# Holding GpSimd back from the values' block until six of the eight normed tiles have their residues

## The chip, the cores and the metric

The kernel runs on one core of a Trainium2 chip. The metric is the device time of one launch in microseconds. Before the change it was 2746.05 us, the median of three runs (2745.25 to 2750.39). The engines that matter here are TensorE (matmuls, PE in the rows), VectorE (DVE), ScalarE (ACT), GpSimd (POOL) and SyncE, which issues the loads (SP).

## The reference, cut to what matters

Two small transformer blocks run one after the other on 512 rows of width 1024, with a context of 256 rows. The change lies at their seam: the last norm of the first block, the modulation of the second block's first layer, and the keys, values and queries of its windowed attention.

```python
def rmsnorm(x, g):
    xf = x.astype(jnp.float32)
    inv = lax.rsqrt(jnp.mean(xf * xf, axis=-1, keepdims=True) + RMS_EPS)
    return (xf * inv).astype(x.dtype) * g
...
    return rmsnorm(x, final_g)            # end of the first block
...
        hx = x * (1.0 + sc1) + sh1
        hc = ctx * (1.0 + csc1) + csh1
...
    q = apply_rope((hx @ wq).reshape(B, L, A_KV_HEADS, G, HEAD_DIM), cos, sin)
    k = apply_rope((hx @ wk).reshape(B, L, A_KV_HEADS, HEAD_DIM), cos, sin)
    v = (hx @ wv).reshape(B, L, A_KV_HEADS, HEAD_DIM)
    kc = (hc @ wk).reshape(B, C, A_KV_HEADS, HEAD_DIM)
    vc = (hc @ wv).reshape(B, C, A_KV_HEADS, HEAD_DIM)
```

## The kernel before, in words

**Products in three parts.** Each float32 product is done as three matmuls on a faster format: every operand is split into a rounded part (hi) and a residue (lo), and hi x hi, lo x hi and hi x lo are summed. The activations live transposed, eight tiles of 128 features by 768 columns (512 rows of x, then 256 of the context), in `Ahi` and `Alo`. The weights stream from HBM in blocks of 128 x 2048, two halves each, into a ring of three slots (`raw`); GpSimd splits each half into `whi` and `wlo` with a multiply (L526) and a subtract (L528). SyncE loads a half into a slot as soon as TensorE has used the half that was there (semaphore `w_used`). The order of blocks on GpSimd is written out by hand in its own program.

**The norm "n5".** VectorE adds the last products of the feed-forward network into X, ScalarE squares X, TensorE sums the squares (L708), ScalarE and VectorE form the root and its inverse (L1342, L1758), and TensorE spreads it over the partitions into PSUM (L718). Then, for k from 0 to 8, VectorE issues in this order: tile k scaled, its 512 columns (L1778, one input from PSUM) and its 256 context columns (L2101, SBUF to SBUF); and the residues of tile k - 1 (L1785, two SBUF inputs, one instruction for 512 and one for 256 columns), for which ScalarE has meanwhile written the rounded part (L1367). The semaphore `n5_out`, on the semaphore that all norms share as `out`, counts the tiles whose residues are written. TensorE's key product (block `B_KV`) waits for it tile by tile. After the eighth tile VectorE goes on, in its own order, with eight pairs of scalings of X (L2106, SBUF to SBUF, and L2107, with an input from PSUM), and with the rotations of the two key heads.

**What follows.** TensorE's key product runs over 8 tiles with the first block of keys (two heads), then the values' product with the block `B_KV + 1`, which needs both halves of that block split. ScalarE copies the keys' halves in swapped order (L1326), and VectorE rotates each head with three instructions: L2113 (an input from PSUM), L2115 and L2118 (two SBUF inputs). When both rotations and ScalarE's copy of the values are done (semaphore `kvA_evac` at 3), TensorE transposes the values (L1040), VectorE copies them out of PSUM (L2128), and only then the query product with the blocks from `B_WQA` starts.

**The places touched.** GpSimd's program calls `split_run(B_KV, ring_end(B_WOA))`: it splits the keys' block, the values' block and five blocks behind them, each as soon as its half has landed. Block `B_KV` has slot 2 of the ring, the values' block slot 0, the first query block slot 1.

Of the kernel before, what the change touches and what calls it, by code (L numbers as in the profile page):

```python
# [28 lines left out]
KT = D // P  # L29
# [87 lines left out]
B_KV = B_FF[1] + FF_BLOCKS  # L117
B_WQA = B_KV + 2
B_WOA = B_WQA + 4
# [50 lines left out]
def build(nc, ins, out):  # L170
    ctx = ExitStack()
    with ctx:
# [51 lines left out]
        def sem(name):  # L224
            name = shared.get(name, (name, 0))[0]
            if name not in sems:
                sems[name] = ctx.enter_context(nc.semaphore(name))
            return sems[name]

        def when(name, count):  # L230

            return sem(name), count + shared.get(name, (name, 0))[1]
# [287 lines left out]
        def _(pool):  # L520
            def split(s, half, loaded, nth):

                part = slice(half * HALF, (half + 1) * HALF)
                pool.wait_ge(*when(f"raw{s}{half}", loaded))
                pool.sem_inc(sem("w_turn"), 1)
                pool.tensor_scalar(whi[:, s, part], raw[:, s, part], 1.0, 1.0, ALU.mult, ALU.mult).then_inc(sem("w_hi"), 1)  # L526
                pool.wait_ge(*when("w_hi", nth))
                pool.tensor_tensor(wlo[:, s, part], raw[:, s, part], whi[:, s, part], ALU.subtract).then_inc(sem("w_split"), 1)  # L528

            def split_block(b, more=0, rounds=0):  # L530

                for half in range(2):
                    split(b % RING, half, 16 * rounds + (16 * (b // RING) + 16), more + (SPLITS[b] + half + 1))

            def split_run(first, end):

                a, z = -(-first // RING), end // RING
                if z - a < 2:
                    for b in range(first, end):
                        split_block(b)  # L540
                    return
                for b in range(first, a * RING):
                    split_block(b)
                with pool.Fori(0, z - a) as i:
                    for s in range(RING):
                        split_block(a * RING + s, 2 * RING * i, i)
                for b in range(z * RING, end):
                    split_block(b)

            def split_swiglu(f):  # L550
                B0 = B_FF[f]
                for b in (B0 + 2, B0 + 3):
                    split_block(b)
                with pool.Fori(0, FF_IT // 3) as p:
                    for s in range(3):
                        for b in (0, 2, 4):
                            split_block(B0 + 4 + 5 * s + b, FF_SPLITS * p, 5 * p)
                for i in range(FF_IT // 3 * 3, FF_IT - 1):
                    for b in (0, 2, 4):
                        split_block(B0 + 4 + 5 * i + b)  # L560
                split_block(B0 + FF_BLOCKS - 1)

            def ring_end(b):
                return -(-b // RING) * RING
# [53 lines left out]
            split_swiglu(0)  # L618
            split_block(B_POOL)
            split_swiglu(1)  # L620
            split_run(B_KV, ring_end(B_WOA))
            for u in range(N_UNITS):
                pool.wait_ge(*when("denA", u + 1))
                prob = probA[u % 4][:, 1:1 + len(keys(UNITS[u][2])) * P]
# [44 lines left out]
        def _(pe):  # L669
# [34 lines left out]
            def quarters(bank, cols, src, k):  # L704

                n = sum(n for _, n in cols) // 4
                for q in range(4):
                    mm = pe.matmul(ps[32 * q:32 * q + 32, bank, 0:n], ones[:, 0:32], src[:, q * n:(q + 1) * n],  # L708
                                   start=(k == 0), stop=(k == KT - 1), skip_group_check=True)
                return mm  # L710

            def spread(bank, cols, src):

                n = sum(n for _, n in cols) // 4
                for q in range(4):
                    a, z = q * n, (q + 1) * n
                    for c0, c1 in ((a, z),) if a // 512 == (z - 1) // 512 else ((a, 512), (512, z)):
                        mm = pe.matmul(psf[:, bank * 512 + c0:bank * 512 + c1], ident[:, 32 * q:32 * q + 1].to_broadcast([P, P]),  # L718
                                       src[:, c0 - a:c1 - a], start=True, stop=True, skip_group_check=True)
                return mm  # L720
# [21 lines left out]
            def dense(name, b0, cols, ready, first_two=True):  # L742


                slots = 8 // len(cols)
                dst = [[ps[:, (j % slots) * len(cols) + c, 0:n] for c, (_, n) in enumerate(cols)] for j in range(8)]
                blocks = [(SPLITS[b0 + i], b0 + i) for i in range(4)]
                for i in ((0, 2, 3) if ready else range(4)):
                    both = bool(ready) and i == 0
                    if 2 * i + 2 > slots:  # L750
                        pe.wait_ge(*when(f"{name}_evac", 2 * i + 2 - slots))
                    columns(f"{name}_done", blocks[i:i + 1 + both], cols, dst[2 * i:], ready if both else None)
# [1753 lines left out]
```

## Time and profile before

| | |
|---|---|
| median of 3 runs | 2746.05 us (2745.25 to 2750.39) |
| the profiled execution, its own time | 2749.13 us |
| its span | 2747.3 us |
| TensorE busy | 2598.0 us, 95% of the span |
| VectorE busy | 1489.6 us, 54% |
| GpSimd busy | 1357.1 us, 49% |
| ScalarE busy | 649.7 us, 24% |
| mean granted clock of TensorE | 0.973 of full speed |

The span runs from the first to the last instruction of the profiled execution; its own time is the device time of that same execution. The busy shares are means over the whole program. The change concerns some 60 us of it, around 1005 to 1065 us, and the rows below are read there: timelines of single engines, with the start, the length and the line of each instruction, and the chain of waits, which follows the work that ended last.

### The profile page before, as it was taken

To read this page: it belongs to the slowest core of one execution; us is meant where nothing else is said; L and a number is where in the kernel's file an instruction comes from. 1 tells how busy PE (TensorE), PEld (TensorE's weight loads), DVE (VectorE), ACT (ScalarE), POOL (GpSimd) and SP (SyncE) were. 2 spreads that over 40 slices of the span, in tenths; PEclk is the share of its full clock that TensorE was granted. 3 is DMA by queue.
4 is the path that set the end of the run, shared out by engine and by line. 5 is a ranking of instruction groups with operands and counts; after the bars stand their busy time and mean duration, and the time that the engine had idled before them with its cause. 6 is when DMAs were issued, how large, how long until landed. Compare 5 with 4: busy or idle time off the path is not lost.

```text
span 2747.3 us, 39149 instructions
## 1 busy us (share of the span) xinstructions
PE 2598.0 (95%) x14176; PEld 2103.1 (77%) x14176; DVE 1489.6 (54%) x2473; ACT 649.7 (24%) x1220; POOL 1357.1 (49%) x880
## 2 busy tenths in 40 slices
PE   7989999989999989889989999999799999899997
PEld 6668777777777768656768888888588887688885
DVE  7945666466566645354454333333676665544444
ACT  2220000041000023567131111111255552211112
POOL 6374565536555554133546444444252525766661
PEclk9999999999999999999999999999899999999998
DMA  5124444434444431000111112111011111232321
GB/s 196 47 78 146 153 153 153 151 118 133 153 153 153 153 123 62 31 1 1 47 39 62 61 63 67 61 61 61 31 47 46 43 34 56 69 98 92 99 92 46
DMA packets 67387, 235.73 MB, mean 86 GB/s; under 512 B 8144, under 2 KB 9552, under 8 KB 67152
## 3 DMA queue, kind: packets, MB, share of 16 engines
q1 hardware_dynamic: 65792, 233.64, 26.1%
q8 instruction: 63, 1.03, 0.2%
q10 hardware_dynamic: 1488, 0.69, 0.1%
q14 instruction: 44, 0.36, 0.0%
HBM read 232.21 MB, written 2.10 MB: 85 GB/s over the span
## 4 chain that ended last, share of the span: by engine, by line
PE 87%; DVE 6%; ACT 3%; issue 2%; POOL 1%; DMA 1%; SPq 0%; DVEq 0%; ACTq 0%; POOLq 0%
PE ps L675 70%; PE ps L1210 2%; PE ps L1233 2%; PE ps L830 2%; PE ps L1172 2%; PE ps L1098 1%; PE ps L1084 1%; PE ps L794 1%; PE ps L1164 1%; PE ps L708 1%; DVE Alo L1785 1%; PE ps L718 1%; DVE tmp L1778 1%; DMA raw<-in_stream 1%; DVE X L1796 1%
## 5 line engine op out<-in xcount | busy, mean ns | idle before, releaser
L526 POOL TENSOR_SCALAR whi<-raw 128x1024 fp32r<-128x1024 f32 x332 | 372.8, 1123 | 1024.4 <-DMA raw<-in_stream 1024.2
L528 POOL TENSOR_TENSOR wlo<-raw,whi 128x1024 fp32r<-128x1024 f32 x332 | 804.3, 2423 | 27.7
L675 PE MATMUL ps<-Ahi,whi 128*128 128x512 f32 (+1 forms) x2128 | 726.6, 373 | 41.6 <-DVE Alo L1785 18.7
L675 PE MATMUL ps<-Alo,whi 128*128 128x512 f32 (+1 forms) x2128 | 719.4, 369 | 0.0
L675 PE MATMUL ps<-Ahi,wlo 128*128 128x512 f32 (+1 forms) x2128 | 717.1, 368 | 0.0
L2222 DVE SCALAR_TENSOR_TENSOR X<-ps,modT,X 128x512 f32<-128x512 f32 (+1 forms) x384 | 242.4, 659 | 504.7 <-PE ps L675 504.7
L675 PEld LDWEIGHTS ps<-Ahi,whi 128*128 128x128 f32 x2128 | 374.9, 190 | 121.3 <-DVE Alo L1785 19.2
L675 PEld LDWEIGHTS ps<-Ahi,wlo 128*128 128x128 f32 x2128 | 374.6, 190 | 68.9
L675 PEld LDWEIGHTS ps<-Alo,whi 128*128 128x128 f32 x2128 | 375.6, 190 | 66.6 <-issue 0.7
L675 PE MATMUL ps<-hhi,whi 128*128 128x512 f32 x1120 | 375.9, 373 | 9.2 <-DVE hlo L2212 8.4
L675 PE MATMUL ps<-hhi,wlo 128*128 128x512 f32 x1120 | 374.8, 372 | 0.0
L675 PE MATMUL ps<-hlo,whi 128*128 128x512 f32 x1120 | 372.5, 369 | 0.0
L675 PEld LDWEIGHTS ps<-hhi,whi 128*128 128x128 f32 x1120 | 193.9, 189 | 53.5 <-DVE hlo L2212 9.2
L675 PEld LDWEIGHTS ps<-hlo,whi 128*128 128x128 f32 x1120 | 193.7, 189 | 39.1
L675 PEld LDWEIGHTS ps<-hhi,wlo 128*128 128x128 f32 x1120 | 193.6, 189 | 39.0
L1326 ACT ACTIVATE hhi<-tmp 128x512 fp32r<-128x512 f32 (+1 forms) x108 | 73.6, 695 | 633.3 <-DVE tmp L2208 472.6
L1994 DVE TENSOR_TENSOR X<-ps,X 128x512 f32<-128x512 f32 x176 | 121.7, 691 | 139.8 <-PE ps L675 139.8
L1970 DVE SCALAR_TENSOR_TENSOR ps<-raw,arena,ps 128x256 f32<-128x256 f32 x432 | 173.9, 480 | 41.4 <-DMA raw<-in_stream 41.4
L1326 ACT ACTIVATE arena<-ps 128x256 f32<-128x256 f32 (+5 forms) x194 | 101.6, 543 | 245.9 <-PE ps L889 67.3
L625 POOL TENSOR_SCALAR tmp<-tmp,sm 128x256 f32<-128x256 f32 (+2 forms) x96 | 63.0, 658 | 148.2 <-DVE sm L2177 148.1
L1476 ACT ACTIVATE tmp<-ps 128x512 f32<-128x512 f32 x44 | 26.3, 598 | 427.0 <-PE ps L675 425.9
L1623 ACT ACTIVATE tmp<-ps 128x512 f32<-128x512 f32 x96 | 47.1, 525 | 290.9 <-PE ps L675 288.6
(300 smaller groups left out, 2864.1 us busy)
## 6 DMA issues: line engine op xcount, KB each, us to landing
raw<-in_stream SPq DMA_DIRECT2D x428, 512.0 KB, 3.8
X<-in_xT SPq DMA_DIRECT2D x2, 1024.0 KB, 6.5
arena<-in_dft SPq DMA_DIRECT2D x1, 2048.0 KB, 16.9
out_xT<-X SPq DMA_DIRECT2D x2, 1024.0 KB, 4.3
X<-in_ctxT SPq DMA_DIRECT2D x1, 1024.0 KB, 19.3
w<-in_stream SPq DMA_DIRECT2D x2, 512.0 KB, 4.2
vec<-in_vec SPq DMA_DIRECT2D x1, 364.5 KB, 7.6
arena<-in_fmap SPq DMA_DIRECT2D x1, 256.0 KB, 12.4
```

The lines of the kernel that those rows point to most:

```text
L526: pool.tensor_scalar(whi[:, s, part], raw[:, s, part], 1.0, 1.0, ALU.mult, ALU.mult).then_inc(sem("w_hi"), 1)
L528: pool.tensor_tensor(wlo[:, s, part], raw[:, s, part], whi[:, s, part], ALU.subtract).then_inc(sem("w_split"), 1)
L625: pool.tensor_scalar(prob, prob, sm[:, u % 8, 2:3], 1.0, ALU.mult, ALU.mult).then_inc(sem("pA"), 1)
L675: mm = pe.matmul(dst[c], w[:, b % RING, off:off + P], rhs(k, part, c0, n), start=(k == 0 and w is whi and part == 0), stop=(k == kn - 1 an ...
L830: mm = pe.matmul(ps[:, WOUT_BANK[j], :], w[:, at:at + P], a[:, k, 0:T], start=(k == 0 and w is hi and a is Ahi), stop=(k == KT - 1 and w i ...
L1172: mm = pe.matmul(ps[:, 6, :], vB[:, t, hh * P:(hh + 1) * P], aT[:, t, :], start=(t == 0), stop=(t == NTT - 1))
L1210: mm = pe.matmul(ps[:, 6 + t % 2, 0:256], a[:, k, t * P:(t + 1) * P], w[:, (B_QKV + 2) % RING, k * 256:(k + 1) * 256], start=(k == 0 and a ...
L1233: mm = pe.matmul(psf[:, a:a + 384], q, kB[hh][t][:, half * 384:half * 384 + 384], start=(part == 0), stop=(part == 1))
L1326: return act.activation(dst, src, ACT.Copy, scale=scale)
L1970: mm = dve.scalar_tensor_tensor(out=to, in0=row, scalar=c, in1=acc, op0=ALU.mult, op1=ALU.add)
L1994: dve.tensor_tensor(X[:, m, 0:T], ps[:, 4 + m % 2, :], X[:, m, 0:T], ALU.add).then_inc(sem(f"{name}_dfree"), 1)
L2222: mm = dve.scalar_tensor_tensor(out=X[:, m, c0:c0 + n], in0=ps[:, 4 + len(cols) * (m % (4 // len(cols))) + c, 0:n], scalar=mod(l, 5, m, c) ...
```

## The change

GpSimd's run of blocks is cut behind its first block. The keys' block is split as before. Then GpSimd waits until `n5_out` stands at KT - 2 = 6, that is, until VectorE has written the residues of six of the eight normed tiles. Then it goes on with the values' block and the rest of the run. No instruction is added but the wait, and no other engine's program is changed.

```diff
             split_swiglu(0)
             split_block(B_POOL)
             split_swiglu(1)
-            split_run(B_KV, ring_end(B_WOA))
+            split_block(B_KV)
+            pool.wait_ge(*when("n5_out", KT - 2))
+            split_run(B_KV + 1, ring_end(B_WOA))
             for u in range(N_UNITS):
                 pool.wait_ge(*when("denA", u + 1))
```

On GpSimd the rows around the cut, before the change: the last block of the feed-forward network (raw10, raw11), the keys' block (raw20, raw21), and the loop over whole turns of the ring, which begins with the values' block (raw00). The name in the brackets is the semaphore that is waited for; raw20 is the first half of slot 2.

```order
L526 TENSOR_SCALAR whi<-raw 128x1024 [waits raw11]
L528 TENSOR_TENSOR wlo<-raw,whi 128x1024 [waits w_hi]
L526 TENSOR_SCALAR whi<-raw 128x1024 [waits raw20]
L528 TENSOR_TENSOR wlo<-raw,whi 128x1024 [waits w_hi]
L526 TENSOR_SCALAR whi<-raw 128x1024 [waits raw21]
L528 TENSOR_TENSOR wlo<-raw,whi 128x1024 [waits w_hi]
L544 UNCONDITIONAL_BRANCH
L544 ISA
L526 TENSOR_SCALAR whi<-raw 128x1024 [waits raw00]
```

The same place after the change:

```order
L526 TENSOR_SCALAR whi<-raw 128x1024 [waits raw11]
L528 TENSOR_TENSOR wlo<-raw,whi 128x1024 [waits w_hi]
L526 TENSOR_SCALAR whi<-raw 128x1024 [waits raw20]
L528 TENSOR_TENSOR wlo<-raw,whi 128x1024 [waits w_hi]
L526 TENSOR_SCALAR whi<-raw 128x1024 [waits raw21]
L528 TENSOR_TENSOR wlo<-raw,whi 128x1024 [waits w_hi]
L544 UNCONDITIONAL_BRANCH [waits out]
L544 ISA
L526 TENSOR_SCALAR whi<-raw 128x1024 [waits raw00]
```

No row has moved: the entry of the loop now carries a wait for the norms' count of residues, and everything behind it on GpSimd stands behind that wait. The line numbers behind the cut are two higher in the changed kernel (L2101 becomes L2103).

## Rows read from the trace of the kernel before

**Rows 1.** The chain of waits from 1005 to 1062 us: start us, us, what.

```profile
1019.46 3.92 DVE Alo L1785 x2
...
1047.42 2.71 DVE arena L2118
...
1052.18 0.89 PE ps L1040 x6
...
1054.10 8.00 PE ps L675 x36
```

**Rows 2.** Timeline of VectorE in the norm: start us, us, engine, line, operation.

```profile
1016.17 0.86 DVE L2101 TENSOR_SCALAR tmp<-X,s 128x256 f32<-128x256 f32 x1
...
1017.60 1.86 DVE L2101 TENSOR_SCALAR tmp<-X,s 128x256 f32<-128x256 f32 x1
...
1023.31 0.73 DVE L1778 SCALAR_TENSOR_TENSOR tmp<-X,s,ps 128x512 f32<-128x512 f32 x1
1023.97 0.34 DVE L2101 TENSOR_SCALAR tmp<-X,s 128x256 f32<-128x256 f32 x1
1024.23 1.13 DVE L1785 SCALAR_TENSOR_TENSOR Alo<-tmp,s,Ahi 128x512 fp32r<-128x512 f32 x2
...
1026.21 1.13 DVE L1785 SCALAR_TENSOR_TENSOR Alo<-tmp,s,Ahi 128x512 fp32r<-128x512 f32 x2
```

**Rows 3.** Timeline of GpSimd beside it.

```profile
1008.95 1.04 POOL L526 TENSOR_SCALAR whi<-raw 128x1024 fp32r<-128x1024 f32 x1
...
1012.40 1.05 POOL L526 TENSOR_SCALAR whi<-raw 128x1024 fp32r<-128x1024 f32 x1
...
1016.97 2.35 POOL L528 TENSOR_TENSOR wlo<-raw,whi 128x1024 fp32r<-128x1024 f32 x1
...
1020.45 2.65 POOL L528 TENSOR_TENSOR wlo<-raw,whi 128x1024 fp32r<-128x1024 f32 x1
```

**Rows 4.** Timeline of ScalarE, in the norm and behind the key product.

```profile
1017.06 1.12 ACT L1367 ACTIVATE Ahi<-tmp,s 128x512 fp32r<-128x512 f32 x2 [4.78 <-DVE tmp L2101]
...
1040.72 5.61 ACT L1326 ACTIVATE arena<-ps 128x256 f32<-128x256 f32 x10 [3.42 <-PE ps L675]
```

**Rows 5.** Timeline of TensorE: start of the key product, start and end of the values'.

```profile
1023.44 1.01 PE L675 MATMUL ps<-Ahi,whi 128*128 128x512 f32 x2 [7.97 <-DVE Alo L1785]
...
1041.56 0.51 PE L675 MATMUL ps<-Ahi,whi 128*128 128x512 f32 x2
...
1049.53 0.51 PE L675 MATMUL ps<-Ahi,wlo 128*128 128x512 f32 x2
```

**Rows 6.** Timeline of VectorE behind the norm.

```profile
1037.33 1.11 DVE L2106 TENSOR_SCALAR X<-X 128x256 f32<-128x256 f32 x1
1038.36 0.73 DVE L2107 SCALAR_TENSOR_TENSOR X<-X,rg,ps 128x512 f32<-128x512 f32 x1
1039.01 1.92 DVE L2106 TENSOR_SCALAR X<-X 128x256 f32<-128x256 f32 x1
...
1042.37 0.28 DVE L2106 TENSOR_SCALAR X<-X 128x256 f32<-128x256 f32 x1
...
1051.43 0.69 DVE L2118 TENSOR_TENSOR arena<-arena 128x512 f32<-128x512 f32 x1
```

**Rows 7.** Timeline of GpSimd beside it.

```profile
1037.24 1.05 POOL L526 TENSOR_SCALAR whi<-raw 128x1024 fp32r<-128x1024 f32 x1 [14.14 <-DMA raw<-in_stream]
1038.37 2.40 POOL L528 TENSOR_TENSOR wlo<-raw,whi 128x1024 fp32r<-128x1024 f32 x1
...
1054.11 1.04 POOL L526 TENSOR_SCALAR whi<-raw 128x1024 fp32r<-128x1024 f32 x1 [4.53 <-DMA raw<-in_stream]
```

**Rows 8.** Timeline of VectorE in the first norm of the program.

```profile
29.81 3.68 DVE L1754 TENSOR_TENSOR Alo<-tmp,Ahi 128x512 fp32r<-128x512 f32 x2
```

**Rows 9.** Timeline of GpSimd beside it.

```profile
31.46 1.49 POOL L526 TENSOR_SCALAR whi<-raw 128x1024 fp32r<-128x1024 f32 x1
```

**Rows 10.** Busy time by stretch: PE, PEld, DVE, ACT, POOL, granted clock.

```profile
1015.50:1023.40 7.90, 0.00 (x0) 0.00 (x0) 7.89 (x7) 2.24 (x4) 7.43 (x5) 0.50 0.00 0
```

## The prediction

> **What bounds the kernel now.** I read three views of the stretch around the norm. The chain of waits comes first [rows 1]: from the spread of the norm's factors, done at 1015.5 us, it runs over VectorE to the first pair of residues (3.92 us for two instructions), stays on VectorE through the residues, the scaling of X and the rotations of the keys, and returns to TensorE at 1052.18 for the values' transposes; the query product starts at 1054.10. So two things are VectorE-bound here: when the key product may start (1023.44, after TensorE stood idle for 7.97 us [rows 5]), and when the query product may start.
>
> The timelines of VectorE and GpSimd, laid side by side, say why VectorE is slow in places. An undisturbed tile costs it 0.66 us for the scaled tile (L1778, from 1023.31 to 1023.97), 0.26 for the context's half (L2101) and 1.06 for the residue pair (L1785): 1.98 us, the distance from one residue pair to the next [rows 2]. Before 1023.38 the same instructions are long: L2101 took 1.86 us and ended at 1019.46, just behind GpSimd's subtract, which ended at 1019.32; the first residue pair took 3.92 us on the chain and ended at 1023.38, 0.28 behind the subtract that ended at 1023.10 [rows 1, 3]. L2106 shows it again later: 1.11 and 1.92 us instead of 0.28, ending 0.15 us behind a GpSimd instruction both times, while L2107, which reads PSUM, took 0.73 beside a running subtract [rows 6, 7]. So VectorE instructions with two SBUF inputs, and the plain SBUF-to-SBUF scalings, wait for the running GpSimd instruction to end; those that read PSUM don't. The other direction costs GpSimd little: behind two queued 512-column VectorE instructions in the first norm, its next multiply took 1.49 us instead of 1.05 [rows 8, 9], so GpSimd got its turn between the two. I carry this further as: at each boundary between two GpSimd instructions about one waiting VectorE instruction gets through, then GpSimd goes on.
>
> **The change part by part.** Nothing is removed and nothing is added but one wait. Behind the keys' block (its last subtract is over at 1008.95 [rows 3]) GpSimd stands until six residue pairs are done. Queued behind it are, in this order, the two halves of the values' block, two halves of the first query block, and, as SyncE's loads land, two halves of the second and two of the third. SyncE is not held: its loads wait for TensorE's use of the ring alone.
>
> Gain at the start. Without a GpSimd instruction beside it VectorE starts at 1015.50 and issues 0.66 + 0.26 + 0.66 + 0.26 us. The first residue pair then needs ScalarE's rounded tile, which starts as the first L2101 ends (about 1016.5) and takes 1.12 us [rows 4], so 1017.7; the pair lasts 1.13 [rows 2], to 1018.8. TensorE starts 0.06 later, at 1018.9 against 1023.44: 4.6 us earlier. The granted clock in the idle stretch before it is 0.50, the lower level, 1.2 GHz [rows 10]; at 1.01 us for its first two matmuls [rows 5] TensorE also starts slowly now. The idle stretch becomes shorter by 4.6, the slow start I leave as it is; below it turns out that this does not matter.
>
> Where the work goes. Residue pairs come every 1.98 us, the sixth at 1018.8 + 5 x 1.98 = 1028.7. GpSimd then starts at about 1029.0: the 0.3 us for the wait, the loop's entry and the wait for the block is my estimate, bounds 0.1 and 1.0 (less than one multiply of 1.05). One half costs 3.45 us (1008.95 to 1012.40 [rows 3]). Eight halves are ready to follow each other: the second query block's halves are loaded after TensorE is half through, and through, the key product, the third's after the values' product; from GpSimd's 1037.24 and 1054.11 [rows 7] and the product's start they come some 4 us behind their release, that is at 1033, 1043.5 and 1051.5 in the new order, each in time but the last, which is some 0.6 us late. That is 8 x 3.45 = 27.6 us in 16 instructions. GpSimd is held at the boundaries where a 512-column instruction of VectorE goes first, by 0.3 to 0.45 us (1.49 - 1.05 [rows 9]) some six times: 2.4 us. It ends at 1029.0 + 27.6 + 2.4 + 0.6 = 1059.6.
>
> VectorE has, behind the sixth pair, 17 instructions that must share with GpSimd: one L2101, two residue pairs (4), eight L2106, and two in each of the two rotations (4). Before, the eight L2106 met only two instructions of GpSimd, because its ring was empty. Now they meet an unbroken row of 16. Each boundary passes one, the first passes two (L2101 and a residue, since L2101 is through in 0.1 us), so VectorE's last add (L2118 of the second rotation) passes as GpSimd's 16th instruction ends, at 1059.6, and is done at 1060.1. Before, it started at 1051.43 and took 0.69: 1052.1 [rows 6]. What follows is the same as before: six transposes, a copy on VectorE, and the query product 1.98 us behind the add (1052.12 to 1054.10 [rows 1]). So the query product starts at 1062.1 instead of 1054.1: **+8.0 us**.
>
> The last two residue pairs fall under the same rule. TensorE spends 2.08 us on a tile of the key product (six pairs of matmuls, 0.347 from one to the next), with its slow start 18.1 us from 1023.44 to 1041.56, and 8.3 to 8.5 on the values' product, to 1050.0 [rows 5]; so the seventh is done at about 1033.0, where TensorE would want it at 1032.8, the eighth at 1037.0 instead of 1034.9. The key product ends at about 1039.2, still 2.3 us earlier than before, and the values' product at 1047.5; both halves of the values' block are split by 1036.8, in time. All this is covered: TensorE then stands for the transposes from 1047.5 to 1060.1. The 4.6 us won at the front are lost in that wait. What comes behind the query product is released by it and moves along with it.
>
> Sum: +8.0 us. The profiled execution before took 2749.13 us with a span of 2747.3, 3.1 above the median of the runs; its sum is 2757.1. Against the median: 2746.05 + 8.0 = 2754.05, rounded **2754.0 us**. The bounds of the unknown terms: if GpSimd starts later, or two VectorE instructions get through at one boundary once more, the last add falls one subtract earlier, 2.4 us: +5.6. If the longer idle stretch before the query product costs TensorE another slow start like the one at 1023.44, it is 1 to 2 us more: +10. If the waits on the boundaries were worth nothing at all: 8 x 0.86 us for L2106 and L2107 behind a last pair at 1032.7 ends at 1039.6, ScalarE's swapped copies end 4.8 us behind the key product as now (1046.3 against 1041.56 [rows 4, 5]), at 1041.8, and the values' product ends at 1045.3; the query product starts at 1048.5, or **-5.6**.
>
> **The rivals.** First: the norm alone decides, and what moves is hidden. The Trainium skill's page SBUF — State Buffer, section "Summary: rules for kernel authors", advises to schedule whichever of the two engines is off the critical path; the change does this for six tiles. Taken from rows, this is the case with the bound just worked out: -5.6 us, 2740.5. For it speaks the idle stretch of 7.97 us, which surely becomes shorter; against it that VectorE is still on the chain of waits after the norm [rows 1] and that L2106 did wait for GpSimd [rows 6].
>
> Second: the waits are fewer than one per boundary. VectorE's L2107 leave GpSimd 0.66 us in which it can start first, but two short instructions might pass at one boundary, or GpSimd might run out of blocks because a load lands late. Each such case takes 1.0 to 2.4 us off; with two or three of them the query product starts 1 to 5 us later than before: about 2749. The section "Who interferes with whom" of the same page says that issue order decides who blocks; were VectorE's next instruction issued first each time, its back-to-back pairs would pass together, which is this rival; the 1.49 us of GpSimd between two queued instructions of VectorE [rows 8, 9] speaks against.
>
> Third, the wait doesn't do what it says: if the count were reached early or GpSimd had nothing to hold back, the trace would stay as it is, 2746. GpSimd's row of instructions from 1008.95 to 1023.10 [rows 3] shows that it has, so I give it next to nothing.
>
> **How the numbers follow.** A measurement of this kernel can tell about 0.2%, 5.5 us, from no change. Forecast, +5.6 to +10: 0.67. Second rival, 0 to +5.5: 0.22. First rival, between -5.6 and 0: 0.07, about half of it a gain too small to tell. More than +10, from a slower clock: 0.04. So faster 0.04, same 0.26, slower 0.70. The range goes from 2748.5 (+2.5, half of the second rival) to 2757 (+11).
>
> **What would show it.** Right: the first residue pair takes 1.13 us and TensorE starts at about 1018.9; no GpSimd instruction between 1008.95 and 1029; eight splits without a gap from there; six or more of the eight L2106 longer than 0.5 us; the transposes at about 1060 and the query product at about 1062. Wrong: L2106 short beside a running GpSimd, or the rotations done by 1052. If the transposes start before 1052 the forecast's sign is wrong.

## The result and the profile after the change

The changed kernel took 2759.89 us, the median of 6 runs (2759.01 to 2763.78), beside 2749.06 us for 6 runs of the kernel before, three more than stood ahead of the prediction. The ratio is 1.0037 with a 95% interval of 1.0026 to 1.0048: 10.2 us slower, between 7.1 and 13.2. The slowdown is clear of the noise, as forecast (+8.0), but the time lies above the range that was given (2748.5 to 2757). All ratios here and below are of fast runs; one of the ten runs of the changed kernel with its scalings moved took 14470 us and is not in its ratio. The profiled execution has a span of 2761.9 us (2747.3 before).

Everything in this profile stands about 1.1 us later than before already ahead of the change's place: the spread of the norm's factors ends at 1016.56 instead of 1015.47. I therefore count from the end of the spread, and call the time from there to the start of the query product the stretch. The chain of waits behind it (start us, us, what):

```profile
1018.79 1.15 DVE Alo L1787 x2
...
1031.40 8.03 DVE Alo L1787 x4
1039.43 2.41 DVE X L2108
...
1060.83 1.55 PE ps L1042 x6
...
1063.42 8.74 PE ps L677 x35
```

The first row answers to the 3.92 us of [rows 1]: the first pair of residues (one instruction for 512 and one for 256 columns of a tile) now takes 1.15 us. The second is new: the residues of the last two tiles, four instructions, take 8.03 us. The query product starts at 1063.42, 46.86 us behind the spread; before it was 38.64. That is +8.2 us in the stretch alone.

The timeline of TensorE (in the brackets its idle time ahead of the instruction, and what ended it):

```profile
1020.00 1.00 PE L677 MATMUL ps<-Ahi,whi 128*128 128x512 f32 x2 [3.44 <-DVE Alo L1787]
...
1035.52 0.62 PE L677 MATMUL ps<-Ahi,whi 128*128 128x512 f32 x2 [0.73 <-DVE Alo L1787]
...
1039.49 0.62 PE L677 MATMUL ps<-Ahi,whi 128*128 128x512 f32 x2 [1.59 <-DVE Alo L1787]
...
1060.83 1.54 PE L1042 MATMUL ps<-ident,tmp 128*128 128x128 f32 x6 [10.47 <-DVE arena L2120]
```

The key product starts after 3.44 us of idle time instead of 7.97 [rows 5], stops for tile 7 and tile 8, and TensorE then stands 10.47 us ahead of the transposes (2.13 before). GpSimd beside it:

```profile
1030.20 1.05 POOL L526 TENSOR_SCALAR whi<-raw 128x1024 fp32r<-128x1024 f32 x1 [20.08 <-DVE Alo L1787]
1031.34 2.40 POOL L528 TENSOR_TENSOR wlo<-raw,whi 128x1024 fp32r<-128x1024 f32 x1
1033.70 1.49 POOL L526 TENSOR_SCALAR whi<-raw 128x1024 fp32r<-128x1024 f32 x1
...
1037.68 1.48 POOL L526 TENSOR_SCALAR whi<-raw 128x1024 fp32r<-128x1024 f32 x1
...
1054.42 1.62 POOL L526 TENSOR_SCALAR whi<-raw 128x1024 fp32r<-128x1024 f32 x1 [2.15 <-DMA raw<-in_stream]
...
1058.76 1.48 POOL L526 TENSOR_SCALAR whi<-raw 128x1024 fp32r<-128x1024 f32 x1
```

It stands 20.08 us, resumes at 1030.20, and works from there to 1062.98 with one gap of 2.15 us. And VectorE behind the norm, first the eight scalings of the context as a group (L2108, which was L2106; busy us, mean ns), then some of them and the last rotation:

```profile
L2108 DVE TENSOR_SCALAR X<-X 128x256 f32<-128x256 f32 x8 | 9.9, 1236 | 0.0
```

```profile
1039.36 2.48 DVE L2108 TENSOR_SCALAR X<-X 128x256 f32<-128x256 f32 x1
...
1042.42 0.48 DVE L2108 TENSOR_SCALAR X<-X 128x256 f32<-128x256 f32 x1
...
1043.47 1.92 DVE L2108 TENSOR_SCALAR X<-X 128x256 f32<-128x256 f32 x1
...
1053.00 0.28 DVE L2108 TENSOR_SCALAR X<-X 128x256 f32<-128x256 f32 x1
...
1057.10 2.23 DVE L2117 TENSOR_TENSOR arena<-arena 128x512 f32<-128x512 f32 x1
1059.43 1.34 DVE L2120 TENSOR_TENSOR arena<-arena 128x512 f32<-128x512 f32 x1
```

The long ones each end just behind a GpSimd instruction: the first at 1041.84, behind the subtract that began at 1039.25 and took 2.44, and the last add passes when the multiply of 1058.76 ends at 1060.24. Only the one at 1053.00, in GpSimd's gap, takes the 0.28 us of [rows 6]. Before, the eight had taken 4.7 us, now 9.9.

### The profile page after: what moved, and what is told of

The parts are those of the page before. It is cut to its first block, busy times and chain, and to the rows that moved or that the text cites. A ratio compares the mean times of both kernels' runs of the same rounds, so it can differ in the third digit from the quotient of the medians.

```text
span 2761.9 us, 39149 instructions
## 1 busy us (share of the span) xinstructions
PE 2608.3 (94%) x14176; PEld 2112.4 (76%) x14176; DVE 1487.5 (54%) x2473; ACT 649.1 (24%) x1220; POOL 1359.1 (49%) x880
## 4 chain that ended last, share of the span: by engine, by line
PE 88%; DVE 7%; ACT 2%; issue 2%; POOL 1%; DMA 1%; SPq 0%; DVEq 0%; ACTq 0%; POOLq 0%
PE ps L677 70%; PE ps L1212 2%; PE ps L1235 2%; PE ps L1100 2%; PE ps L832 2%; PE ps L1174 1%; PE ps L1086 1%; PE ps L796 1%; DVE Alo L1787 1%; PE ps L1166 1%; PE ps L710 1%; PE ps L1061 1%; DVE tmp L1780 1%; DMA raw<-in_stream 1%; PE ps L720 1%
```

## The experiments

Two theories. **Boundaries:** a VectorE instruction with two SBUF inputs, or a plain SBUF-to-SBUF scaling, waits until GpSimd's running instruction ends, and one passes per boundary between two GpSimd instructions. What the change moved is GpSimd's row of splits: before, eight such instructions waited for it; in its new place seventeen stand beside it, and fifteen wait (all but a scaling and a multiply of the rotation). **Lateness:** the loss comes from GpSimd, or TensorE behind it, getting its blocks later. The table has all kernels; the times against the kernel before are worked out from the ratio to its runs on the same chip (median 2751 us; 2749 for the first measurement), and the last column is read from the profiles.

| kernel | expected, us | measured, us (95%) | spread to query product, us |
|---|---|---|---|
| before (three profiles) | | | 38.64, 38.36, 38.30 |
| changed (four profiles) | | +10.2 (+7.1 to +13.2) | 46.86, 46.86, 46.89, 46.88 |
| waits for eight tiles | 0 to +2 | +5.0 (+1.7 to +8.5) | 39.70 |
| wait behind the values' block | +1 to +2 | +6.1 (+2.2 to +9.6) | 40.02 |
| changed, scalings later | -1 to -3 | -2.2 (-6.1 to +1.7) | 37.01 |
| before, scalings later | -1 | -2.2 (-5.8 to +1.4) | 37.38 |
| query blocks held, scalings later | -5 to -6 | -5.2 (-7.7 to -2.5) | 33.30 |
| query blocks held | -5 to -6 | -5.2 (-8.0 to -2.8) | 33.73 |
| changed, scalings read PSUM | +1 to +3 | +1.7 (-1.1 to +4.4) | 39.72 |
| changed, again | +8 to +9 | +9.9 (+6.3 to +13.2) | 46.86 |

**Waiting for all eight tiles.**

```diff
-            pool.wait_ge(*when("n5_out", KT - 2))
+            pool.wait_ge(*when("n5_out", KT))
```

> The changed kernel, but GpSimd waits for all eight tiles' residues instead of six, so it resumes about 4 us later. Theory (each VectorE instruction with two SBUF inputs or a plain SBUF scaling waits for the end of a running GpSimd instruction): the last two residue pairs and the last context scaling run undisturbed, five waits fewer; the key product ends at about 21.5 us behind the end of the norm's spread (changed kernel 26), the values' product waits some 2 us for its block, the query product starts about 39 us behind the spread, as before the change (38.6), against 46.8 in the changed kernel; time 0 to +2 us against before. Rival (what costs is that GpSimd gets to the blocks late): 4 us later still, so +12 to +14 us against before.

VectorE's last two residue pairs, and TensorE's two stops, in the timelines of this kernel:

```profile
1030.89 2.42 DVE L1787 SCALAR_TENSOR_TENSOR Alo<-tmp,s,Ahi 128x512 fp32r<-128x512 f32 x4
```

```profile
1020.21 1.01 PE L677 MATMUL ps<-Ahi,whi 128*128 128x512 f32 x2 [3.44 <-DVE Alo L1787]
...
1040.75 0.62 PE L677 MATMUL ps<-Ahi,whi 128*128 128x512 f32 x2 [1.84 <-POOL wlo L528]
...
1054.03 1.39 PE L1042 MATMUL ps<-ident,tmp 128*128 128x128 f32 x6 [4.54 <-DVE arena L2120]
```

The four instructions take 2.42 us instead of 8.03 and the key product runs through; the values' product then waits 1.84 us for its block, as expected. The query product comes 39.7 us behind the spread, 7.2 less than in the changed kernel, though GpSimd resumes 3.3 us later. The rival asked for the opposite. In the ratio the kernel is +5.0 us; the expected +2 at most lies just inside the interval. The rival's +12 to +14 us lie outside it. That this kernel is faster than the changed one is shown by the stretch alone, since the intervals of the two whole times overlap. The whole time is some 4 us more than the stretch explains, and the profile can't say where: its own execution took 2748.94 us, 6 us less than the median of this kernel's runs.

**The wait one block later.** Here GpSimd splits the values' block at once and is held only ahead of the first query block.

```diff
             split_block(B_KV)
+            split_block(B_KV + 1)
             pool.wait_ge(*when("n5_out", KT - 2))
-            split_run(B_KV + 1, ring_end(B_WOA))
+            for b in range(B_KV + 2, ring_end(B_WOA)):
+                split_block(b)
```

> The wait for six tiles stands one block later, behind the values' block, so only four halves' worth of splits are held back up to the third query block's loads, not six. Theory: GpSimd is done with the values' block just as the norm's spread ends; it has six halves to split behind the sixth pair, two with gaps for loads; the last residue pairs still wait (key product ends as in the changed kernel, 26 us behind the spread), but the scalings of X meet a GpSimd that runs out of blocks: the query product starts about 40 us behind the spread, +1 to +2 us against before. Rival (the loss comes from the values' block being late for TensorE): all of it goes, the gain of the norm stays, -4 to -5 us.

```profile
1031.38 8.12 DVE L1789 SCALAR_TENSOR_TENSOR Alo<-tmp,s,Ahi 128x512 fp32r<-128x512 f32 x4
...
1042.49 0.28 DVE L2110 TENSOR_SCALAR X<-X 128x256 f32<-128x256 f32 x1
...
1047.85 1.92 DVE L2110 TENSOR_SCALAR X<-X 128x256 f32<-128x256 f32 x1
```

```profile
1039.31 2.45 POOL L528 TENSOR_TENSOR wlo<-raw,whi 128x1024 fp32r<-128x1024 f32 x1
1045.98 1.16 POOL L526 TENSOR_SCALAR whi<-raw 128x1024 fp32r<-128x1024 f32 x1 [4.21 <-DMA raw<-in_stream]
1047.22 2.40 POOL L528 TENSOR_TENSOR wlo<-raw,whi 128x1024 fp32r<-128x1024 f32 x1
1054.32 1.04 POOL L526 TENSOR_SCALAR whi<-raw 128x1024 fp32r<-128x1024 f32 x1 [4.70 <-DMA raw<-in_stream]
```

The last residues still take 8.12 us, but then GpSimd runs out of loaded blocks (4.21 us ahead of 1045.98), and five of the scalings take 0.28 us. 40.0 us to the query product, expected 40; the rival's -4 to -5 is excluded. The ratio is again some 4 us above the stretch, which stays unexplained.

**The scalings of the context moved behind the copy of the values**, in the changed kernel and in the kernel before.

```diff
             for k in range(KT):
-                dve.tensor_scalar(X[:, k, T:TT], X[:, k, T:TT], ALPHA, None, ALU.mult)
                 dve.scalar_tensor_tensor(out=X[:, k, 0:T], ...
...
             dve.tensor_copy(vA.rearrange("p t d -> p (t d)"), ...
+            for k in range(KT):
+                dve.tensor_scalar(X[:, k, T:TT], X[:, k, T:TT], ALPHA, None, ALU.mult)
```

> The changed kernel, with VectorE's eight scalings of the context in X (L2108 there) moved behind its copy of the values, where it waits for TensorE anyway. Theory: eight of the seventeen waits leave the path; the rotations start about 27 us behind the spread instead of 37, the query product 37 us behind it instead of 46.8: -1 to -3 us against before, some 10 under the changed kernel. Rival (the path goes through GpSimd's splits themselves, or through ScalarE's copies): within 1 us of the changed kernel, +8 to +10 against before.

> The kernel before, with the same eight scalings of the context moved behind VectorE's copy of the values. Theory: only two of the eight waited for GpSimd there (2.5 us), and the values' product and ScalarE's copy of it are next at 1051.0 against the rotations' end of 1052.1, so the query product starts only 1 us earlier: -1 us, no change that can be measured. Rival (the scalings are worth their whole 3.9 us on the path): -3 to -4 us.

In the changed kernel the eight instructions that are left (they read PSUM) run through beside GpSimd's splits without a stop, and the rotations begin 28.1 us behind the spread instead of 37.3:

```profile
1041.42 5.34 DVE L2108 SCALAR_TENSOR_TENSOR X<-X,rg,ps 128x512 f32<-128x512 f32 x8
1046.69 0.68 DVE L2114 SCALAR_TENSOR_TENSOR arena<-ps,arena 128x512 f32<-128x512 f32 x1
```

The query product comes 9.9 us earlier than in the changed kernel. So the path did go through those eight small instructions. In the kernel before the same move gives 0.9 to 1.3 us in the stretch; ScalarE's copy of the values, which ends 35.4 us behind the spread, is then the last thing that the transposes (35.5) wait for. Both ratios lie near their expectation, and neither can be told from no change.

**The eight scalings with an operand in PSUM.** These add the norm's factor to the context, which the reference doesn't; everything else is the changed kernel.

```diff
-                dve.tensor_scalar(X[:, k, T:TT], X[:, k, T:TT], ALPHA, None, ALU.mult)
+                dve.scalar_tensor_tensor(out=X[:, k, T:TT], in0=X[:, k, T:TT], scalar=ALPHA, in1=norm_scale("n5", 0, C),
+                                         op0=ALU.mult, op1=ALU.add)
```

> The changed kernel with its eight SBUF-to-SBUF scalings of the context replaced, in the same place, by scale-and-add instructions of the same size whose second input lies in PSUM (they add the norm's factor to the context, which the reference doesn't). GpSimd's program and the order on VectorE are those of the changed kernel; each of the eight takes some 0.4 us instead of 0.28 when alone. Theory (what waits is the kind of operand): the eight take 0.4 us each beside a running GpSimd instead of 0.5 to 2.5, the query product starts about 40 us behind the spread instead of 46.8: +1 to +3 us against before, in spite of longer instructions. Rival (VectorE waits for something else, the number of instructions or GpSimd's progress): they are as long as in the changed kernel, +8 to +10.

```profile
L2108 DVE SCALAR_TENSOR_TENSOR X<-X,ps 128x256 f32<-128x256 f32 x8 | 3.3, 409 | 0.0
```

```profile
1043.01 0.41 DVE L2108 SCALAR_TENSOR_TENSOR X<-X,ps 128x256 f32<-128x256 f32 x1
...
1044.00 0.41 DVE L2108 SCALAR_TENSOR_TENSOR X<-X,ps 128x256 f32<-128x256 f32 x1
```

```profile
1042.36 1.05 POOL L526 TENSOR_SCALAR whi<-raw 128x1024 fp32r<-128x1024 f32 x1
1043.49 2.40 POOL L528 TENSOR_TENSOR wlo<-raw,whi 128x1024 fp32r<-128x1024 f32 x1
```

These instructions are longer than an undisturbed scaling, and yet all eight take 0.41 us with GpSimd at work beside them; the one at 1044.00 lies wholly inside the subtract of 1043.49 to 1045.89. The mean is 409 ns against 1236 in the changed kernel. The query product comes 7.1 us earlier. GpSimd's program, the order and the number of instructions are unchanged, so what decides is the kind of instruction. The operation was changed together with its operand here; that it is the operand follows from the same operation elsewhere in these profiles: the residues (SCALAR_TENSOR_TENSOR too, both inputs in SBUF) wait, 8.03 us for four, and the scalings of the 512 columns (one input in PSUM) don't, 0.73 us beside a running subtract [rows 6, 7]. This is the test that the boundary theory could have failed most plainly.

**A version from the findings.** GpSimd splits the keys' and the values' block at once (it is done with them 1.2 and 1.4 us behind the end of the spread), holds the first query block until the norm is over, and the second until the rotations and ScalarE's copy of the values are done; once with VectorE's scalings moved, once without.

```diff
             split_block(B_KV)
+            split_block(B_KV + 1)
+            pool.wait_ge(*when("n5_out", KT))
+            split_block(B_KV + 2)
+            pool.wait_ge(*when("kvA_evac", 3))
+            for b in range(B_KV + 3, ring_end(B_WOA)):
+                split_block(b)
```

> A version built from the findings: GpSimd splits the keys' and the values' block without a wait, then waits for all eight residues before the first query block, and for the rotations and ScalarE's copy of the values before the second; and VectorE's eight scalings of the context stand behind its copy of the values. Theory: nothing on VectorE's path meets GpSimd except two residues or rotations beside the first query block; the key product starts 3.5 us behind the spread and ends 21.5 behind it, the values' product 29.9, the query product 33 us behind it, against 38.6 before and 46.8 in the changed kernel: -5 to -6 us against before. Rival (GpSimd's lateness costs): the second query block's split, now some 8 us later, holds TensorE in the query product, and the time is that of before or above.

> The same two waits on GpSimd, VectorE's program as before the change. Theory: the eight scalings meet only the first query block's four instructions, four waits; they end at about 27.7 us behind the spread, the rotations at 31, just as ScalarE's copy of the values does; the query product again starts 33 us behind the spread, -5 to -6 us against before. Rival (the scalings must leave the path for any gain): 1 to 3 us slower than the version that moves them.

The version without the move, VectorE's scalings, of which four wait:

```profile
1032.50 0.65 DVE L2112 TENSOR_SCALAR X<-X 128x256 f32<-128x256 f32 x1
...
1033.71 1.93 DVE L2112 TENSOR_SCALAR X<-X 128x256 f32<-128x256 f32 x1
...
1036.22 0.48 DVE L2112 TENSOR_SCALAR X<-X 128x256 f32<-128x256 f32 x1
...
1037.27 1.93 DVE L2112 TENSOR_SCALAR X<-X 128x256 f32<-128x256 f32 x1
...
1039.78 0.28 DVE L2112 TENSOR_SCALAR X<-X 128x256 f32<-128x256 f32 x1
```

With the move, the same instructions wait behind VectorE's copy, where nobody waits for them:

```profile
1044.97 10.39 DVE L2135 TENSOR_SCALAR X<-X 128x256 f32<-128x256 f32 x8
```

Both are faster than the kernel before (ratio 0.9981 each, 0.9972 to 0.9991 and 0.9971 to 0.9990), and thus than the changed kernel too. Both reach the query product 33 to 34 us behind the spread; moving the scalings gains 0.4 us there and nothing that the times can tell. The second query block's split, which starts 31.6 and 32.0 us behind the spread, kept TensorE waiting in neither. Both also start the query product at the full granted clock: its thirteenth pair of matmuls begins 4.3 us behind its first, against 5.7 to 5.8 in the three profiles of before.

**The changed kernel again, and what the stretch leaves open.**

> The changed kernel itself once more, on this chip, for the part of its loss that the stretch behind the norm doesn't show (+8.2 us there, +10.2 by the ratio). Theory (the rest is scatter of the later stages, by TensorE's granted clock): the stretch to the query product is again 46.8 us, and the ratio lies at +8 to +9 us. Rival (the later start of the query product costs another 2 us or more in the stages behind it, each time): the ratio is again +10 us or more.

> The changed kernel, one more profile. Theory (the 2 us of loss outside the stretch behind the norm are scatter of TensorE's granted clock in the attention): the stretch to the query product is 46.8 us again, and the attention's 175 to 179 us differ from the two profiles at hand (179.3 both). Rival (the later start makes the attention lose them each time): the attention takes 179 us again.

> The same as the profile before it, a second time: 46.8 us to the query product; an attention between 174 and 179 us by the theory, 179 again by the rival.

> The kernel before, one more profile. 38.6 us from the spread to the query product. Theory: the attention, 175.1 us in the one profile at hand, comes out elsewhere between 173 and 179. Rival: it stays at 175.

> The kernel before, once more: 38.6 us to the query product; the attention between 173 and 179 us by the theory, 175 again by the rival.

The stretch repeats to 0.03 us in four profiles of the changed kernel. The rest does not. The attention, from the first to the last transpose of its probabilities, took 175.1, 175.2 and 177.1 us in the three profiles of before, and 179.3, 179.3, 177.2 and 179.3 in the four of the changed kernel. The stage in one row each (from and to, length; PE, PEld, DVE, ACT, POOL busy; the last column but two is the granted clock), first two of the kernel before, then two of the changed one:

```profile
1135.50:1310.60 175.10, 158.88 (x1125) 105.88 (x1124) 87.08 (x224) 125.38 (x328) 64.06 (x97) 0.96 0.00 1
```

```profile
1136.00:1313.10 177.10, 161.04 (x1125) 107.79 (x1124) 87.18 (x224) 125.30 (x328) 64.06 (x97) 0.95 0.00 1
```

```profile
1145.60:1324.90 179.30, 163.38 (x1125) 109.56 (x1124) 87.17 (x225) 125.06 (x328) 64.01 (x97) 0.93 0.00 1
```

```profile
1145.60:1322.90 177.30, 161.02 (x1126) 108.11 (x1124) 87.28 (x225) 125.39 (x328) 64.38 (x97) 0.94 0.00 1
```

VectorE's, ScalarE's and GpSimd's busy times are alike in all four; what goes with the length is the granted clock, 0.96, 0.95, 0.93 and 0.94. So the extra time of that stage goes with more time at the lower level, 1.2 GHz. Neither expectation holds cleanly: the stage isn't 179 us each time, as the rival had it, but no profile of the changed kernel has it shorter than any of the kernel before (177.2 against 177.1 at the closest), and the means differ by 3 us. The profiles of the seven variants speak for the rival too: the same stage takes 173.7 to 176.9 us in them. So in all ten profiles in which the query product starts 33 to 40 us behind the spread the attention is shorter than in each of the four in which it starts at 46.9. That the changed kernel loses time there is therefore hardly chance; what lowers the clock there stays open. The ratio of the second measurement is +9.9 us, between the two expectations, and its interval holds both.

## Why the prediction was wrong

The mechanism and the sign were right, and so was the sum of the stretch (+8.0 forecast, +8.2 measured, in four profiles alike). The time left the range for reasons that lie outside the stretch. The error is 5.9 us (2759.89 against 2754.0), in these parts:

- **"Against the median: 2746.05 + 8.0".** This is the step that put the time outside the range. The median of three runs was taken as if it were known. Six runs have 2749.06, 3.0 us more; 31 runs beside the first experiments had 2750.8, from 2742.4 to 2755.9. This is half of the error, and the range held nothing for it: its top was 2746.05 + 11, and the same 11 us on top of 2749.06 would have held the measured time. The prediction's own sum from the profiled execution, 2757.1, had already reached that top.
- **"What comes behind the query product is released by it and moves along with it."** This term was put at nothing, and it failed too. It is the rest of the error, 2.6 us by the medians (10.8 - 8.2) and 2.0 by the ratio (10.2 - 8.2; 1.7 the second time). The intervals reach 3 us each way, so the whole times alone don't show it; the profiles do, in two places. The query product's thirteenth pair of matmuls begins 6.6 us behind its first in the four profiles of the changed kernel, and 5.7 to 5.8 in the three of before: some 0.85 us for a longer time at the lower clock. And the attention runs 3 us longer on average, at a lower granted clock, for a reason that stays open. I had allowed a slow start of 1 to 2 us, and only at the query product.
- **The term itself**, +8.0: 0.2 us short.

Within the term, step by step, behind the spread: the key product's start was forecast at 3.4 us and came at 3.44. GpSimd resumed at 13.6 (forecast 13.5), 0.36 us behind the sixth residue pair. That "the first passes two" was wrong: the last context scaling took it alone, each of the four residues needed a boundary of its own, and the eighth pair was ready 22.9 us behind the spread, not 21.5. The values' product ended 1.8 us later than forecast for that, so the third query block landed later and GpSimd stood 2.15 us, not 0.6. In this gap and at its end a scaling and a multiply of the rotation passed freely, and the last add went by at the end of GpSimd's fifteenth instruction, 43.7 us behind the spread, instead of its sixteenth at 44.1. These errors nearly cancel, so that the term is off by only 0.2 us is partly luck. The transposes then took 1.55 us on the chain instead of 0.89 [rows 1], at the lower clock:

```profile
1016.60:1020.00 3.40, 0.00 (x1) 0.01 (x1) 3.13 (x7) 2.13 (x4) 0.00 (x0) 0.50 0.00 0
1020.00:1024.00 4.00, 4.00 (x12) 3.42 (x13) 4.00 (x9) 2.24 (x4) 0.00 (x0) 0.50 0.00 0
...
1060.80:1063.40 2.60, 1.54 (x6) 1.14 (x6) 0.96 (x1) 0.00 (x0) 2.18 (x1) 0.50 0.00 0
1063.40:1068.40 5.00, 4.98 (x15) 4.31 (x16) 0.00 (x0) 0.00 (x0) 0.00 (x0) 0.50 0.00 0
```

The granted clock was at its lower level, 0.50, through the idle time ahead of the key product and for 4 us into it; cutting the idle time from 7.97 to 3.44 us did not spare TensorE the slow start. That I had left it as it is was right; that the query product's slow start would last 5 us after the longer wait, with 3.4 us at a mean clock of 0.55 before, was in the upper bound only.

The rivals: the first (the norm alone decides, -5.6) is excluded by the result; it has, though, the size of what the version from the findings gains (-5.2), in which the held splits come back where few or none of VectorE's instructions on the path stand beside them. The second (fewer waits than one per boundary) did not happen: seven of the eight scalings waited. My sign of being right, six or more of them longer than 0.5 us, was badly put and is missed: four are longer, and three that wait for a multiply rather than a subtract take 0.47 to 0.48. The Trainium skill's page SBUF — State Buffer, section "Who interferes with whom", says that the loser blocks for the whole instruction, and that an instruction of VectorE with at most one SBUF input outside its two-port modes does not contend; the traces agree, with 1.92 us beside 0.28 for the scalings and 409 ns for those with an operand in PSUM.

## What to carry to other kernels

Where instructions of two engines wait for each other, holding one engine back does not remove its work from the path, it moves it. List what will run beside it in its new place, and count how many instructions of the other engine must pass. In a row of long instructions, a short one of the kind that waits costs the time to the next boundary, whatever its own length, so many small ones on the path are the worst neighbours. Move them behind a wait that they don't end; and where the same work can be written with one operand in PSUM, it did not wait here. For a change of 0.3%, take the baseline's own scatter and the granted clock of the later stages into the range, and judge the mechanism by a stretch between two events in the profile.

## What the runs showed of the hardware that was not expected

The two engines alternated at the boundaries even when both had instructions queued: two residue instructions in a row never passed together (8.03 to 8.12 us for four in three kernels, against 2.42 undisturbed). GpSimd paid little: its multiply of 1.05 us became 1.09 beside a 256-column scaling and 1.48 to 1.49 beside a 512-column instruction. And TensorE's granted clock was at the lower level, 0.50, after an idle time of 3.44 us just as after one of 7.97.
